# The order of three masks, a sum and a weight split in the triangular inverse of a two-model kernel

## The reference

```
def step(S, inp):
    r_t, w_t, k_t, v_t, kk_t, a_t = inp
    sa = jnp.einsum('bhij,bhj->bhi', S, -kk_t)
    S = (S * w_t[:, :, None, :]
         + sa[..., None] * (kk_t * a_t)[:, :, None, :]
         + v_t[..., None] * k_t[:, :, None, :])
    y = jnp.einsum('bhij,bhj->bhi', S, r_t)
    return S, y
```

## Time and profile before

| | |
|---|---|
| median of three runs | 1010.65 us (1007.94, 1010.65, 1011.37) |
| the profiled execution | 1011.37 us, of which its span is 1009.5 us |
| PE busy | 942.1 us, 93% of the span |
| DVE busy | 574.7 us, 57% |
| ACT busy | 452.3 us, 45% |
| POOL busy | 74.9 us, 7% |
| PE's share of the chain that ended last | 85% |
| mean granted clock of PE | 0.977 of full speed |

### The profile page before, as it was taken

The page is one execution under the profiler, slowest core; times in us unless marked ns, Lnnn a source line. Parts: engine busy times, 40 slices in busy tenths (PEclk is TensorE's granted clock), DMA queues, the critical chain, the costliest instruction groups (busy, mean ns, idle before and its releaser), DMA issues.

```text
span 1009.5 us, 16945 instructions
## 1 busy us (share of the span) xinstructions
PE 942.1 (93%) x7262; PEld 847.1 (84%) x7262; DVE 574.7 (57%) x706; ACT 452.3 (45%) x621; POOL 74.9 (7%) x150
## 2 busy tenths in 40 slices
PE   4999999998979998999899999997999699999995
PEld 3898889998779987887689999996985589999994
DVE  4456677556567767735475555546541865555553
ACT  5445555434356644430264444444521654435441
POOL 6000000000120012000000000000542000000000
PEclk9999999999899999989999999998999899999998
DMA  9754444556544551000155565654772156556521
GB/s 304 241 172 147 146 144 150 167 169 207 178 151 150 181 168 43 2 1 2 43 167 195 188 202 168 203 184 130 222 225 79 61 177 201 188 191 202 170 84 42
DMA packets 105642, 152.52 MB, mean 151 GB/s; under 512 B 4050, under 2 KB 82272, under 8 KB 105568
## 3 DMA queue, kind: packets, MB, share of 16 engines
q1 hardware_dynamic: 101120, 141.45, 43.2%
q0 software_dynamic: 4272, 9.85, 3.5%
q10 hardware_dynamic: 176, 0.14, 0.0%
HBM read 145.58 MB, written 1.06 MB: 145 GB/s over the span
## 4 chain that ended last, share of the span: by engine, by line
PE 85%; DVE 5%; ACT 4%; issue 3%; DMA 1%; POOL 0%; POOLq 0%; SPq 0%; ACTq 0%; DVEq 0%
PE banks L1671 23%; PE banks L1672 23%; PE banks L1673 23%; PE banks L2006 4%; PE banks L2205 3%; DVE wl L1035 2%; ACT wh L625 1%; PE banks L2094 1%; DMA raw<-in_w_in 1%; PE banks L1784 1%; DVE xl L1083 1%; PE banks L2105 1%; DMA arena<-in_l_rel_bias 1%; PE banks L1808 1%; PE banks L1759 1%
## 5 line engine op out<-in xcount | busy, mean ns | idle before, releaser
L1035 DVE TENSOR_TENSOR wl<-raw,wh 128x2048 fp32r<-128x2048 f32 x132 | 302.4, 2292 | 176.2 <-ACT wh L625 175.1
L1671 PE MATMUL banks<-xh,wh 128*128 128x256 f32 x1216 | 344.9, 284 | 2.8 <-DVE xl L1083 2.6
L1672 PE MATMUL banks<-xl,wh 128*128 128x256 f32 x1216 | 342.3, 282 | 0.0
L1673 PE MATMUL banks<-xh,wl 128*128 128x256 f32 x1216 | 342.0, 281 | 0.0
L625 ACT ACTIVATE wh<-raw 128x2048 fp32r<-128x2048 f32 x132 | 252.2, 1912 | 137.5 <-PE banks L1673 133.8
L1671 PEld LDWEIGHTS banks<-xh,wh 128*128 128x128 f32 x1216 | 230.3, 189 | 9.0 <-issue 7.8
L1672 PEld LDWEIGHTS banks<-xl,wh 128*128 128x128 f32 x1216 | 230.0, 189 | 1.4 <-issue 0.2
L1673 PEld LDWEIGHTS banks<-xh,wl 128*128 128x128 f32 x1216 | 230.4, 189 | 0.0
L1671 PE MATMUL banks<-wh,yh 128*128 128x512 f32 x288 | 114.7, 398 | 3.0 <-DVE yl L1519 3.0
L1673 PE MATMUL banks<-wh,yl 128*128 128x512 f32 x288 | 113.4, 394 | 0.0
L1672 PE MATMUL banks<-wl,yh 128*128 128x512 f32 x288 | 113.4, 394 | 0.0
(11 more groups left out here) (311 smaller groups left out, 1062.3 us busy)
## 6 DMA issues: line engine op xcount, KB each, us to landing
raw<-in_l_ffn_up SPq DMA_DIRECT2D x32, 1024.0 KB, 5.4
raw<-in_l_ffn_down SPq DMA_DIRECT2D x32, 1024.0 KB, 5.0
raw<-in_w_in SPq DMA_DIRECT2D x29, 1024.0 KB, 5.3
raw<-in_l_w_in SPq DMA_DIRECT2D x13, 1024.0 KB, 5.2
raw<-in_l_pw SPq DMA_DIRECT2D x12, 1024.0 KB, 5.5
arena<-arena POOLq DMA_DIRECT2D x64, 71.0 KB, 3.2
raw<-in_w_out SPq DMA_DIRECT2D x4, 1024.0 KB, 5.1
raw<-in_l_w_out SPq DMA_DIRECT2D x4, 1024.0 KB, 5.2
```

Of the source, the lines that this page charges most:

```text
L1035: nc.vector.tensor_tensor(wl[:, u % WBUFS, :], raw[:, u % RAWS, :], wh[:, u % WBUFS, :].bitcast(F32), ALU.subtract).then_inc(E("lo_split"), 1)
L1671: mm(out, hh, mh, start=start, stop=False)
L1672: mm(out, hh, ml, start=False, stop=False)
L1673: return mm(out, hl, mh, start=False, stop=stop)
```

## The change

Three edits, all in the order of the work.

1. In the table `INVERSE`, `GN` comes ahead of `GA`. This holds for PE's products, for the banks that the steps take, and for DVE's masks. The wait on `ZZ` of the pair before moves with the first step.
2. The identity sum of a group (L1447 before, L1426 after) moves from behind the `GD` masks of the pair to right behind the `GN` masks of its own group. Its wait is now one on DVE's own counter (`dve_steps`).
3. DVE's `next_unit()` that stood behind the sums of pair 0 moves ahead of the whole table, in front of the waits for `band_ready` and the first product.

```diff
--- before.py
+++ after.py
@@ -106,7 +106,7 @@
 
 
 
-INVERSE = [("GA", "dve"), ("GN", "dve"), ("GD", "dve"), ("AV", "act"), ("N2", "act"), ("D2", "dve"),
+INVERSE = [("GN", "dve"), ("GA", "dve"), ("GD", "dve"), ("AV", "act"), ("N2", "act"), ("D2", "dve"),
            ("N4", "act"), ("X2", "dve"), ("D4", "act"), ("X4", "dve"), ("D8", "act"), ("X8", "dve"),
            ("Z1", "act"), ("EZ", "act"), ("ZZ", "dve")]
 
@@ -1377,6 +1377,7 @@
                 nc.vector.tensor_tensor(bonus[:, 512 * i:512 * i + 512], bank(f"bo{i}"), slot(2)[:, 512 * i:512 * i + 512],
                                         ALU.mult).then_inc(empty(f"bo{i}"), 1)
 
+            next_unit()
             dve.wait_ge(E("band_ready"), 1)
             wait_empty(dve, "bo1")
             wait_full(dve, "nat_bn1")
@@ -1415,13 +1416,16 @@
                         use = f"{name}_{g}"
                         ts = tset[g % 2]
                         wait_full(dve, use)
-                        if name == "GA":
+                        if name == "GN":
                             if pair:
                                 wait_empty(dve, f"ZZ_{g - 2}")
-                            masked(ts[3], use, "up32")
-                        elif name == "GN":
                             masked(ts[0], use, "up16", last=False)
                             masked(ts[2], use, "cross")
+                            sync()
+                            idb = ident.rearrange("p (o t) -> p o t", o=1).broadcast_to([P, 4, P])
+                            nc.vector.tensor_tensor(four(ts[4]), four(ts[0]), idb, ALU.add).then_inc(E("series_begun"), 1)
+                        elif name == "GA":
+                            masked(ts[3], use, "up32")
                         elif name == "GD":
                             masked(ts[1], use, "low16")
                         elif name == "D2":
@@ -1439,14 +1443,6 @@
                                                     bank(use).rearrange("p (h w d) -> p h w d", h=4, w=2),
                                                     ts[0].rearrange("p (h w d) -> p h w d", h=4, w=2), ALU.add)\
                                 .then_inc(empty(use), 1)
-                    if name == "GD":
-                        for g in (2 * pair, 2 * pair + 1):
-                            ts = tset[g % 2]
-                            wait_empty(dve, f"GN_{g}")
-                            idb = ident.rearrange("p (o t) -> p o t", o=1).broadcast_to([P, 4, P])
-                            nc.vector.tensor_tensor(four(ts[4]), four(ts[0]), idb, ALU.add).then_inc(E("series_begun"), 1)
-                        if pair == 0:
-                            next_unit()
                     heads_between(len(INVERSE) * pair + i)
 
             nc.vector.memset(S(0), 0.0).then_inc(E("state_zeroed"), 1)
```

## The result

The changed kernel took 1016.77 us (median of six runs, 1015.36 to 1019.52) against 1011.01 before (median of six), which is 0.57% more. The ratio 1.0076, interval 1.006 to 1.0091, is that of all 23 runs of it, whose median is 1018.94 us. Either way it is slower, clear of what counts as noise here, and above my range (1008.8 to 1015.8); I had forecast +0.22%. The profiled execution took 1019.34 us, its span is 1017.5.

What follows compares the result with a forecast made beforehand. PE held 85% of the chain, so only its standstills or lower clock counted; DVE was late at pair 0's hole. Terms -0.15 + 0.6 + 1.3 + 0.5 = +2.25 us took the median from 1010.65 to 1012.9, range 1008.8 to 1015.8.

Steps and rivals of the forecast that it cites:

- DVE's chain in pair 0: Pair 0: split starts 376.90 behind ACT's, first mask 3.27 us later than before, first GD mask done at 386.33.
- The order at full clock: Pair 0: hole ahead of N4 vanishes, waits come further ahead; transposes at 393.91 against 394.06, so -0.15 us.
- I take 0.6: Pair 0: PE's granted clock falls between about 378 and 386.4, costing 0.6 us, bounds 0 and 1.5.
- Over `GD` and `AV` they cost nothing: Pair 0: 1.2 GHz there is free, since AV ends about 385.7 and N2 starts 386.43; over N2 up to about 1.0.
- One chance in three: Pair 1: clock may fall between 414.9 and 418.45, priced 1.5 us, booked as +0.5, bounds 0 and 1.5.
- 1.3 us of order: Pair 1: masks and sums in the new order start N2 1.51 us later; the pair costs +1.3 us.
- the rival's price: POOL blocks DVE's split and sums in pair 0: up to +2.7 us on DVE's path, 1015.4 in all; chance 10%.
- the rival's three meetings: Pair 0: split behind L573 +0.79, first sum behind L578 up to +1.4, second sum behind an L581 step about +0.5.
- The signs of being wrong: Split starting ahead of 376, sum or split a microsecond longer, or pair 0's transposes over 2 us off 393.9.
- The third edit's other ends at nothing: Split about 7 us earlier lets SP load that raw buffer earlier, costed at nothing; DVE's own-counter wait also costs nothing.
- Pair 1 as PE's own chain from `N4` on: Everything behind N4 of pair 1, to 443.9 and into the scan, is PE's chain and moves with it.

Runs made afterwards that it cites:

- e4: Changed kernel with products that nobody reads put into PE's pauses in both pairs; 1013.39 us against 1011.33 for the kernel before, ratio 1.0026.
- e10: Changed kernel with PE's pauses filled in pair 0 only and POOL's three steps held until the sums are done; 1015.17 us against 1012.33 before, ratio 1.0028.
- e2: Changed kernel with DVE's split put back behind the GD masks of pair 0; 1014.28 us against 1011.33 for the kernel before, ratio 1.0023.
- e3: Changed kernel with POOL's three steps held until both sums of pair 0 are done; 1016.97 us against 1011.33 for the kernel before, ratio 1.0054.
- e9: Changed kernel with DVE's split moved from ahead of the table to behind the Z1 step; 1013.51 us against 1012.33 for the kernel before, ratio 1.0015.
- e1: Kernel before with only DVE's split moved ahead of the table, masks and sums in old order; 1014.29 us against 1011.33, ratio 1.0025.
- e5: Kernel before with 12 products that nobody reads in PE's hole ahead of N4 of pair 0; 1011.29 us against 1011.7, ratio 0.9997.
- e6: Kernel before with DVE's split of pair 0 moved behind the Z1 step; 1006.74 us against 1011.7, ratio 0.9953.
- e7: Kernel before with the split behind Z1 and the identity sums behind the D2 copies in both pairs; 1008.74 us against 1011.7, ratio 0.9963.
- e11: Same kernel as e7, measured again; 1004.99 us against 1012.33 for the kernel before, ratio 0.9935.
- e8: Changed kernel itself, measured and profiled again; 1019.04 us against 1011.7 for the kernel before, ratio 1.0077.
- e12: Kernel before, measured and profiled again; 1012.22 us against 1012.33, ratio 1.0001.

## Why the prediction was wrong, point by point

- **DVE's chain in pair 0: right, but for POOL.** The split started behind ACT's, the first mask 4.54 us behind PE's first product (computed 4.53). The first `GD` mask was done 12.34 us behind that product (computed 386.33 - 374.77 = 11.56); most of the difference is the sum that POOL held up.
- **The order at full clock: about right, compared with the wrong number.** I computed 393.91 - 374.77 = 19.14 us for A. e4, at full clock, took 20.04 with POOL's hold of 0.94 and 0.17 of filling in it, so the order alone takes 18.9; e10 gives 18.8. But I set my 19.14 against the 19.29 of the profile, of which 1.6 was a fall of the clock that the second profile of before doesn't have. Against 17.68 the order costs 1.25 us, where I had written -0.15. The step that priced that fall as the kernel's own was wrong.
- **"I take 0.6" for the clock in pair 0: this step failed most.** I said that the clock would fall, but sized the fall by the one in the earlier trace rows, 3.4 us long and partly over idle stretches, and capped it at 1.5. It lasted 13.7 us in both profiles of the changed kernel, over `GD`, `AV`, `N2` and `D2`. "Over `GD` and `AV` they cost nothing" was wrong as well: at 1.2 GHz these products ran on until `N2` started at 392.36, 1.61 us later than the `GD` mask, done at 390.60, and the 0.15 behind it would have let it. `N2` and `D2` then took 6.01 us up to `N4`, computed 3.74. Together that is 3.9 us. e4 takes it away: 23.76 - 20.04 = 3.72 us, and 3.89 with the filling's 0.17.
- **"One chance in three" in pair 1: failed.** The clock fell in all six unfilled profiles with edit 2 (changed twice, e2, e3, e9, e10) and in none of the seven without it (before twice, e1, e5, e6, e7, e11). The price in the changed kernel is 1.6 us: the second `AV` and `N2` took 1.26 + 3.10 us from start to start where 0.93 + 1.85 were needed before. The rest of C's +2.86 is 1.3 us of order, as computed: counted from the pair's first product, `N2` starts 1.85 us later than before, 1.52 without the slowed `AV` (computed 1.51). e4 alone doesn't size this stage.
- **POOL: I gave the hold 10% and put it at nothing in the sum, and it was there, though smaller than the rival's price.** The sum was held 0.94 us in both profiles. Of the rival's three meetings one took place: the split took 2.45 us beside the last step of L573, where 2.29 are usual with POOL idle, and the second sum took 0.68. The Trainium skill (SBUF — State Buffer, "Who interferes with whom") has an exclusive lock between a two-input instruction of the vector engine and an instruction of GpSimd that reads SBUF; I set it aside for a sum that had lost 0.16 us. The traces here agree with the page for POOL's tensor_tensor: L578 took 3.82 instead of 2.36 us behind the split, and the sum 1.63 instead of 0.69 behind L578. They do not agree for POOL's tensor_scalar steps (L573, L581), which read SBUF too: the split started in the middle of one and lost 0.16 us. So the 0.16 us came from a meeting with the kind of step that doesn't block, and was no evidence about L578. (In e10 the L1133 that ended 0.02 us after POOL's L579 has one input in SBUF, not two.)
- **The signs of being wrong.** The split did not start early. The sum took 0.94 us more, and PE's transposes came at 402.01, 23.75 us behind the first product where 19.14 was computed: 4.6 us late. `N2`, computed at 11.66 us behind the first product, came at 14.10.
- **The third edit's other ends at nothing: holds.** The scan takes 12.06 us with the earlier load as without it; in the rest, which varies by up to 2.7 us, nothing of it can be seen. The edit's cost is the delay of the masks and the fall of the clock behind it: e1's A is 20.94 against 17.68 of before without a fall. e6 shows what the place was worth: later instead of earlier takes 2.4 us out of the hole.
- **Pair 1 as PE's own chain from `N4` on: right.** The stretch from there to the scan is 22.06 or 22.07 us in every trace.

Put together: order 1.25 + POOL 0.94 + clock 3.89 in pair 0, order 1.28 + clock 1.58 in pair 1 make 8.94 us against an execution of the kernel before without falls there; the forecast had -0.15, 0, 0.6, 1.3 and 0.5 for the same terms. The medians differ by less, 5.8 us in the first measurement and 7.3 in e8. That the kernel before has falls in some executions could explain it, but how often it has them I can't say from two profiles, so the gap between 8.94 and the medians stays open. Why the clock stays down for 13.7 us in one kernel and 3.4 in another is not settled either.

## What to carry to other kernels

Ahead of a product that the tensor engine awaits, put nothing on the vector engine that nobody awaits yet: a split that is needed over 60 us later goes into idle time behind the chain, even if an idle slot seems to lie in front of it. Here one long pause of PE was not worse than several short ones; before trading them, count what the products behind them would cost at 1.2 GHz, for the whole of them, and whether they would then end later than what comes next is ready. Time lost beside one kind of instruction says nothing of another kind. And take a second profile before a fall of the clock is booked as part of the kernel.

## What the runs showed of the hardware

- The clock fell behind pauses of PE of 0.40 and 1.09 us (e2), and did not in one of two executions with a pause of 3.15 us or 3.17 (before and e12).
- Once down, it stayed down for up to 13.7 us with PE busy in full for the last 10.2 of them (changed kernel), and for 10.24 us in e1 with PE busy throughout.
- Products that nobody reads made the changed kernel 3.7 us faster in pair 0 (e4).
- POOL's tensor_tensor of 128x1024 held up some of DVE's instructions that started beside it: the sum, with both inputs in SBUF, by 0.94 us in the changed kernel, and L1133 by 1.07 in e10. It was itself held 1.46 us by the split. DVE's masks, with one input in PSUM and one in SBUF, ran beside it in their usual 0.68 us.
- POOL's tensor_scalar steps of 128x256 cost DVE far less: 0.16 us for the split that started in one (2.45 against 2.29), and 0.16 for the sum at 382.20 in the kernel before (0.85 against 0.69).
